# Projection's head: x turned, scaled and split tile by tile, beside the projection of its rows

## The chip, the cores and the metric

The kernel runs on one core of a Trainium2 chip. The metric is the device time of one execution in microseconds (us). The engines are TensorE (PE; its weight loads are shown as PEld), VectorE (DVE), ScalarE (ACT), GpSimd (POOL) and SyncE (SP), each with its own instruction stream; they wait for one another by semaphores. DMA queues move data between HBM and the on-chip memory (SBUF); matmul results lie in eight banks of PSUM.

## The reference

One inference step of one layer of a decoder: 512 prompt tokens and 8 x 8 sample tokens, 1024 channels.

```
h = rms_norm(x, g_attn) @ w_in        # 1024 -> 1816 columns
q, kv_c, kv_s, kv_w, gates, u = split(h)
# compressed, selected and window attention on q and kv (with paged caches),
# gated and added; trailing means of u through w_pool; joined
y = x + mix @ w_out
y = y + square(relu(rms_norm(y, g_mlp) @ w_up)) @ w_down
out = rms_norm(y, g_final)            # beside the new kv rows and states

def rms_norm(x, g):
    return x * rsqrt(mean(x * x) + eps) * g
```

Everything is 32-bit. The part that matters here is the first line: `rms_norm` and the columns kv_c, kv_s, kv_w and the gates of `w_in`.

## The kernel before

The work is staged: projection, compression of cached blocks, prompt attention, sample attention, MLP. The change lies in the head of the projection, the function `project`, and each engine's part of it is a nested function (`on_sync`, `on_scalar`, `on_vector`, `on_tensor`) whose order of writing is the order of execution on that engine.

The 576 tokens are five tiles: four of 128 prompt tokens and one of 64 sample tokens. x arrives with tokens on the partitions; matmuls need channels there. So PE turns each tile by 8 transposes of 128 channels each (L779), four into each of two banks of `pb[0]` to `pb[3]`. ACT keeps the first four channel groups in `hT` (L513) and DVE the other four (L643).

A product of 32-bit numbers is made of three matmuls in a shorter format (fp32r): each operand is split into a high half (a copy by ACT) and a low half (what is left, a subtraction by DVE), and high by high, high by low and low by high are added in one bank. Split are x times its gamma (`pxh` by L488, `pxl` by L571; one instruction each for a channel group k over all 576 tokens) and the weights of the row columns, which come in two groups: a (384 columns) and b (408). Group a comes as two loads of four channel groups, `rows_araw`; L484 makes `rows_ah`, L566 `rows_al`, one instruction for each half. The gammas come as rows (`colrows`), are turned by PE (L784) and kept by DVE (L647) as `cols`.

`project_rows(r)` (L753) projects one token tile on one column group: r = 0 to 4 are the five tiles on group a, r = 5 to 9 on group b. It is called pass r here; it has 8 channel groups of 3 matmuls and fills bank `pb[4 + r % 4]`. Pass 4 takes the bank of pass 0 and therefore waits for ra_kept, which says that ACT has kept the rows of tile 0:

```
if r - 4 < TILES:
    pe.wait_ge(ra_kept, r - 3)
```

The factor 1/sqrt(mean(x * x) + eps) (`rstd`) is applied when the rows are kept: `keep_rows` on ACT for group a (L505, L506), on DVE for group b (L585 to L588). It comes from five squares with a sum on ACT, one for each tile (`square`, L479), a mean on DVE (L659), a square root on ACT (L535, with a table load ahead of it) and a reciprocal on DVE (L661). ACT does the squares of tiles 0 and 1 between the turned tiles, the other three behind the last split of x, and then the split of group b's first half ahead of keep_rows(0).

After group a PE sums a diagonal of rstd into all partitions (L793), projects group b, and then eight units of 128 columns (u and q) for all tokens at once (L766). SP issues the loads in the order written; the load of u's columns (`u_raw`, L425) takes x's place and waits for all five squares and all turned tiles.

Of the kernel before, what the change touches and what calls it, by code (L numbers as in the profile page):

```python
# [217 lines left out]
def place_project(nc, m):  # L218

    sb, a = placer(nc), addresses()  # L220
    low, zone = a["low"], a["zone"]
    m.x = sb("px", zone, [P, TILES, D])
    m.xh = sb("pxh", zone + 5120, [P, KT_D, TOK], F32R)
    m.xl = sb("pxl", a["mixT"], [P, KT_D, TOK], F32R)
    m.rows_h = [sb("rows_ah", low, [P, KT_D, RA], F32R), sb("rows_bh", low + 6144, [P, KT_D, RB], F32R)]
    m.rows_l = [sb("rows_al", low + 3072, [P, KT_D, RA], F32R), sb("rows_bl", zone + 9728, [P, KT_D, RB], F32R)]
    m.rows_raw = [sb("rows_araw", zone + 12992, [P, KT_D, RA]), sb("rows_braw", zone + 16064, [P, KT_D, RB])]
    m.junk = sb("pjunk", zone + 19328, [P, D])
    slots = [zone + 19328] + [low + 2048 * s for s in range(3)]
# [130 lines left out]
def project(nc, m, sems, sem):  # L360
# [12 lines left out]
    raw_turned, xt_act, xt_dve = sem("raw_turned"), sem("xt_act"), sem("xt_dve")  # L373
    xh_ready, xl_ready, wh_ready, wl_ready = sem("pxh_ready"), sem("pxl_ready"), sem("pwh_ready"), sem("pwl_ready")
    UNIT0 = 4
# [16 lines left out]
    NU = 8  # L392

# [11 lines left out]

    def on_sync(sp):
        sp.dma_start(m.consts[:, 0:P], m.c_small[:, 0:P]).then_inc(ident_in, 16)
        for i in range(PTILES):
            sp.dma_start(m.x[:, i, :], m.x_prompt[0, P * i:P * i + P, :]).then_inc(x_in[i], 16)
        sp.dma_start(m.x[NS:P, PTILES, :], m.x_sample.rearrange("b t d -> (b t) d")).then_inc(x_in[PTILES], 16)  # L410
# [3 lines left out]
        wv = m.w_in_d[0].rearrange("(k p) n -> p k n", p=P)  # L414
        for c, (a, b) in enumerate(((KV0, KV0 + RA), (KV0 + RA, U0))):
            for h in range(2):
                sp.dma_start(m.rows_raw[c][:, 4 * h:4 * h + 4, :], wv[:, 4 * h:4 * h + 4, a:b])\
                  .then_inc(rowsw_in[c][h], 16)
            if c == 0:
                sp.dma_start(m.consts[:, P:], m.c_small[:, P:]).then_inc(sems.const_in, 16)  # L420
# [9 lines left out]
        sp.wait_ge(wl_ready, 4)  # L430
# [46 lines left out]
    def on_scalar(act):  # L477
# [4 lines left out]
        def split_rows(c, h):  # L482
            act.wait_ge(rowsw_in[c][h], 16)
            act.activation(m.rows_h[c][:, 4 * h:4 * h + 4, :], m.rows_raw[c][:, 4 * h:4 * h + 4, :], ACT.Copy)\  # L484
               .then_inc(wh_ready, 1)

        def split_x(k):
            act.activation(m.xh[:, k, :], m.hT[:, k, :], ACT.Identity, scale=ga[:, k:k + 1]).then_inc(xh_ready, 1)  # L488
# [20 lines left out]

        act.wait_ge(norm_step, CLEAR)  # L510
        for i in range(TILES):
            act.wait_ge(raw_turned, 2 * i + 1)
            act.activation(m.hT[:, 0:4, P * i:P * i + rows(i)],  # L513
                           pb[(2 * i) % 4][:, :].rearrange("p (k t) -> p k t", k=4)[:, :, 0:rows(i)], ACT.Copy)\
               .then_inc(xt_act, 1)
            if i < 2:
                if i:
                    act.wait_ge(ss_ready, i)
                square(i)
        act.wait_ge(cols_step, COLS_KEPT)  # L520
        act.wait_ge(xt_act, TILES)
        split_x(0)
        split_rows(0, 0)
        for k in range(1, 4):
            split_x(k)
        act.wait_ge(xt_dve, TILES)
        split_x(4)
        split_rows(0, 1)
        for k in range(5, KT_D):
            split_x(k)  # L530
        for i in range(2, TILES):
            act.wait_ge(ss_ready, i)
            square(i)
        act.wait_ge(norm_step, VAR)
        act.activation(rstd, var, ACT.Sqrt).then_inc(norm_step, 1)  # L535
        split_rows(1, 0)
        act.wait_ge(norm_step, RSTD)
        keep_rows(0)
        split_rows(1, 1)
# [21 lines left out]
    def on_vector(dve):  # L561
        steps = 0

        def split_rows(c, h):
            dve.wait_ge(wh_ready, 2 * c + h + 1)
            dve.tensor_tensor(m.rows_l[c][:, 4 * h:4 * h + 4, :], m.rows_raw[c][:, 4 * h:4 * h + 4, :],  # L566
                              m.rows_h[c][:, 4 * h:4 * h + 4, :].bitcast(F32), ALU.subtract).then_inc(wl_ready, 1)

        def split_x(k):
            dve.wait_ge(xh_ready, k + 1)  # L570
            dve.scalar_tensor_tensor(out=m.xl[:, k, :], in0=m.hT[:, k, :], scalar=ga[:, k:k + 1],  # L571
                                     in1=m.xh[:, k, :].bitcast(F32), op0=ALU.mult, op1=ALU.subtract)\
               .then_inc(xl_ready, 1)
# [67 lines left out]
        for i in range(TILES):  # L641
            dve.wait_ge(raw_turned, 2 * i + 2)
            dve.tensor_copy(m.hT[:, 4:8, P * i:P * i + rows(i)],  # L643
                            pb[(2 * i + 1) % 4][:, :].rearrange("p (k t) -> p k t", k=4)[:, :, 0:rows(i)])\
               .then_inc(xt_dve, 1)
        dve.wait_ge(cols_step, COLS_TURNED)
        dve.tensor_copy(m.cols[:, :], pb[7][:, 0:20]).then_inc(cols_step, 1)  # L647
        dve.wait_ge(xt_act, TILES)
        dve.wait_ge(xt_dve, TILES)
        dve.wait_ge(cols_step, COLS_KEPT)  # L650
        split_x(0)
        split_rows(0, 0)
        for k in range(1, 5):
            split_x(k)
        split_rows(0, 1)
        for k in range(5, KT_D):
            split_x(k)
# [9 lines left out]
        split_rows(1, 0)  # L667
        split_rows(1, 1)
# [65 lines left out]
    def on_tensor(pe):  # L734
        def project_rows(r):

            c, i = r // TILES, r % TILES
            t0 = P * i if i < PTILES else TOK - P
            if r >= 4:
                if r - 4 < TILES:  # L740
                    pe.wait_ge(ra_kept, r - 3)
                else:
                    pe.wait_ge(rb_rows, r - 3 - TILES)
            n = (RA, RB)[c]
            for k in range(KT_D):
                if r == 0:
                    pe.wait_ge(xl_ready, k + 1)
                if i == 0 and k % 4 == 0:
                    pe.wait_ge(wl_ready, 2 * c + k // 4 + 1)
                xh, xl = m.xh[:, k, t0:t0 + P], m.xl[:, k, t0:t0 + P]  # L750
                wh, wl = m.rows_h[c][:, k, :], m.rows_l[c][:, k, :]
                for part, (x, w) in enumerate(((xh, wh), (xh, wl), (xl, wh))):
                    last = pe.matmul(pb[4 + r % 4][:, 0:n], x, w, start=(k == 0 and part == 0),  # L753
                                     stop=(k == KT_D - 1 and part == 2))
            last.then_inc(rows_mm, 1)
# [13 lines left out]

        pe.wait_ge(ident_in, 16)  # L770
        for u in range(2 * TILES):
            i, kk = u // 2, u % 2
            if kk == 0:
                pe.wait_ge(x_in[i], 16)
            if u >= 4:
                pe.wait_ge((xt_act, xt_dve)[kk], i - 1)
            lo = first(i)
            for k in range(4):
                last = pe.transpose(pb[u % 4][:, P * k:P * k + rows(i)],  # L779
                                    m.x[lo:P, i, P * (4 * kk + k):P * (4 * kk + k) + P], ident[lo:P, lo:P])  # L780
            last.then_inc(raw_turned, 1)

        pe.wait_ge(cols_step, COLS_IN)
        pe.transpose(pb[7][:, 0:20], m.colrows[:, :], ident[0:20, 0:20]).then_inc(cols_step, 1)  # L784
        for r in range(TILES):
            if r == 3:
                pe.wait_ge(cols_step, COLS_KEPT)
            project_rows(r)
        pe.wait_ge(sems.cleared, 2)
        pe.wait_ge(rb_step, DIAG)  # L790
        pe.wait_ge(xt_act, TILES)
# [59 lines left out]
def compress(nc, m, sems, sem):  # L851
# [1334 lines left out]
```

## Time and profile before

| | us |
|---|---|
| median of 3 runs | 901.14 |
| lowest and highest | 899.55, 901.77 |
| the profiled execution's own time | 906.76 |
| its span, first to last instruction | 904.9 |
| PE busy in the span | 827.1 |
| DVE busy | 418.0 |
| ACT busy | 335.5 |

The profile is of one execution. All times in it count from the start of the span, and its durations belong to the 906.76, not to the median. "PEclk" or the clock column is the clock granted to PE: 1.00 is 2.4 GHz, 0.50 is 1.2 GHz. A row of a timeline gives start, duration, engine, line, operation, what is written and read, the count, and in brackets how long the engine was idle before and what ended that.

### The profile page before, as it was taken

The page shows a single profiled execution, that of the slowest core. Times are in us where ns is not written, and L with a number is a line of the kernel's source. Part 1 is how long each engine was busy: PE and PEld are TensorE (multiplying, and loading weights), DVE is VectorE, ACT ScalarE, POOL GpSimd, SP SyncE. Part 2 cuts the span into 40 slices and gives each one's busy share as a digit, 9 for nine tenths or more (in the row PEclk, how much of TensorE's full clock was granted, in tenths as well). Part 3 has the DMA queues.
Part 4 walks back from the last instruction along what each step waited for, and adds up shares of the span by engine and source line. Part 5 has one row for each costly group of instructions (what it writes and reads, how often), then busy time and mean ns, then how long its engine had stood idle before and what let it go on. Part 6 is the DMA issues. An engine that isn't in the chain of part 4 may idle for free.

```text
span 904.9 us, 18147 instructions
## 1 busy us (share of the span) xinstructions
PE 827.1 (91%) x7775; PEld 755.0 (83%) x7775; DVE 418.0 (46%) x782; ACT 335.5 (37%) x626; POOL 135.2 (15%) x160
## 2 busy tenths in 40 slices
PE   5999998987888867786999999999999999999995
PEld 4999977775555645465999999999999999999995
DVE  5435646664555475565327433344333433243432
ACT  6511155552566565463225431133212331043311
POOL 0001101100785345520220000000000000000120
PEclk8999999998899889896999999999999999999998
DMA  8912638932461206526221122222221122222002
GB/s 299 323 72 95 192 78 243 302 120 93 140 204 32 83 1 234 208 62 176 94 93 47 50 90 93 93 93 93 93 84 38 63 93 93 93 94 93 1 1 105
DMA packets 48793, 103.03 MB, mean 114 GB/s; under 512 B 7498, under 2 KB 19166, under 8 KB 46429
## 3 DMA queue, kind: packets, MB, share of 16 engines
q1 hardware_dynamic: 41821, 68.61, 22.9%
q0 software_dynamic: 6912, 33.56, 10.9%
q8 instruction: 45, 0.74, 0.3%
q14 instruction: 15, 0.12, 0.0%
HBM read 97.75 MB, written 8.53 MB: 117 GB/s over the span
## 4 chain that ended last, share of the span: by engine, by line
PE 55%; DVE 3%; issue 2%; POOL 2%; DMA 1%; ACT 1%; another core or an unknown queue 1%; SPq 0%; DVEq 0%; ACTq 0%; POOLq 0%
PE banks L1846 51%; PE banks L1662 1%; DMA low<-in_w_out 1%; POOL rowsT L1437 1%; POOL zone L1437 1%; DVE qT L1560 0%; PE banks L2068 0%; PE banks L1730 0%; DVE qT L1561 0%; PE banks L1651 0%; DVE qT L1568 0%; DVE zone L1572 0%; DVE qT L1565 0%; PE banks L1632 0%
## 5 line engine op out<-in xcount | busy, mean ns | idle before, releaser
L1846 PE MATMUL banks<-xh,wh 128*128 128x288 f32 x640 | 139.0, 299 | 5.4 <-DVE xl L1838 5.0
L1846 PE MATMUL banks<-xl,wh 128*128 128x288 f32 x640 | 138.6, 299 | 0.0
L1846 PE MATMUL banks<-xh,wl 128*128 128x288 f32 x640 | 138.5, 298 | 0.0
L1826 ACT ACTIVATE wh<-low 128x1024 fp32r<-128x1024 f32 x72 | 75.0, 1049 | 109.8 <-PE banks L1846 102.8
L1846 PE MATMUL banks<-ah,wh 128*128 128x288 f32 x512 | 110.1, 297 | 0.0
L1846 PEld LDWEIGHTS banks<-xh,wh 128*128 128x128 f32 x640 | 104.6, 191 | 6.2 <-issue 3.2
L1846 PE MATMUL banks<-ah,wl 128*128 128x288 f32 x512 | 109.7, 296 | 0.0
L1846 PE MATMUL banks<-al,wh 128*128 128x288 f32 x512 | 109.6, 296 | 0.0
L1846 PEld LDWEIGHTS banks<-xl,wh 128*128 128x128 f32 x640 | 104.8, 192 | 0.0
L1846 PEld LDWEIGHTS banks<-xh,wl 128*128 128x128 f32 x640 | 104.6, 191 | 0.0
L1993 DVE TENSOR_TENSOR hT<-banks,hT 128x288 f32<-128x288 f32 x64 | 26.3, 453 | 138.8 <-PE banks L1846 138.8
L1831 DVE TENSOR_TENSOR wl<-low,wh 128x1024 fp32r<-128x1024 f32 x72 | 87.4, 1216 | 5.1 <-ACT wh L1826 5.1
L1846 PEld LDWEIGHTS banks<-ah,wl 128*128 128x128 f32 x512 | 82.5, 189 | 0.0
L1846 PEld LDWEIGHTS banks<-al,wh 128*128 128x128 f32 x512 | 82.4, 189 | 0.0
L1846 PEld LDWEIGHTS banks<-ah,wh 128*128 128x128 f32 x512 | 82.4, 189 | 0.0
L1933 ACT ACTIVATE mixT<-mixT 128x576 f32<-128x576 f32 x32 | 22.0, 687 | 152.1 <-DVE mixT L1989 152.1
L1989 DVE SCALAR_TENSOR_TENSOR mixT<-banks,mixT 128x288 f32<-128x288 f32 x64 | 26.3, 453 | 103.6 <-PE banks L1846 103.4
L1902 POOL TENSOR_TENSOR mixT<-mixT,low 128x576 f32<-128x576 f32 x6 | 9.6, 1592 | 406.0 <-ACT low L1944 406.0
L963 DVE TENSOR_TENSOR blkl<-banks,blkh 128x512 fp32r<-128x512 f32 x64 | 41.2, 685 | 18.9 <-ACT blkh L920 18.7
L1154 ACT ACTIVATE zone<-banks,small 128x512 f32<-128x512 f32 (+3 forms) x64 | 33.2, 523 | 31.3 <-DVE small L1190 31.0
L920 ACT ACTIVATE blkh<-banks 128x512 fp32r<-128x512 f32 x64 | 34.8, 598 | 25.2 <-PE banks L1029 25.2
L1140 POOL TENSOR_SCALAR zone<-zone,small,gates 128x512 f32<-128x512 f32 (+3 forms) x64 | 39.0, 618 | 32.7 <-DVE small L1196 32.3
(341 smaller groups left out, 1374.0 us busy)
## 6 DMA issues: line engine op xcount, KB each, us to landing
low<-in_w_up SPq DMA_DIRECT2D x8, 2048.0 KB, 8.2
low<-in_w_down SPq DMA_DIRECT2D x8, 2048.0 KB, 7.8
zone<-in_cmp_w SPq DMA_DIRECT2D x16, 256.0 KB
o_swin<-in_state_win SPq DMA_DIRECT2D x8, 504.0 KB
px<-in_x_prompt SPq DMA_DIRECT2D x4, 512.0 KB, 5.2
u_raw<-in_w_in SPq DMA_DIRECT2D x1, 2048.0 KB, 10.0
q_raw<-in_w_in SPq DMA_DIRECT2D x1, 2048.0 KB, 10.3
low<-in_state_win SPq DMA_DIRECT2D x4, 512.0 KB
```

Of the source, the lines that this page charges most:

```text
L920: act.activation(m.blkh[u % RING][:, r, :], pb[4 + 2 * (u % 2) + r][:, :], ACT.Copy).then_inc(blk_hi, 1)
L963: dve.tensor_tensor(m.blkl[u % RING][:, r, :], pb[4 + 2 * (u % 2) + r][:, :], m.blkh[u % RING][:, r, :].bitcast(F32), ALU.subtract).then_i ...
L1140: last = pool.tensor_scalar(m.cp[v % 4][:, g, 0:width(v)], m.cp[v % 4][:, g, 0:width(v)], su(v)[:, g:g + 1], m.gates[:, tile(v), a:a + 1], ...
L1154: last = act.activation(m.cp[v % 4][:, g, 0:width(v)], pb[2 * (v % 2) + g][:, 0:width(v)], ACT.Exp, bias=nm(v)[:, g:g + 1], scale=-1.0, ac ...
L1437: pool.tensor_tensor(m.sp[n % 2][:, 512 * x:512 * x + 512].rearrange("p (m b q) -> p m b q", m=4, b=8), bigconst(m, "s_slc")[:, 512 * x:51 ...
L1826: act.activation(wcols(m.wh, i), raw_cols(i), ACT.Copy).then_inc(wh_ready, 1)
L1831: dve.tensor_tensor(wcols(m.wl, i), raw_cols(i), wcols(m.wh, i).bitcast(F32), ALU.subtract)\
L1846: last = pe.matmul(out(i, hf), w[wi], half(x[:, k, :], hf), start=first and part == 0, stop=end and part == 2)
L1902: pool.tensor_tensor(sqsum, sqsum, m.sq[n % 2], ALU.add).then_inc(sq_added, 1)
L1933: act.activation(m.act[i % 2], m.relu[i % 2], ACT.Square).then_inc(a_ready, 1)
L1989: op = dve.scalar_tensor_tensor(out=half(m.relu[i % 2], hf), in0=out(i, hf), scalar=0.0, in1=half(m.rb, hf), op0=ALU.max, op1=ALU.mult)
L1993: op = dve.tensor_tensor(h, out(i, hf), h, ALU.add)
```

## The change

On PE, tile 0 is turned, then the gammas, then tile 1; after that each pass r of group a is followed by the turning of tile r + 2, up to tile 4. ACT keeps both banks of a turned tile (tile 0's second half is kept by DVE). DVE multiplies the whole tile by the gammas into `xg`, which takes the room of mixT; ACT copies it to `pxh`, DVE subtracts into `pxl`, for all 8 channel groups of one tile in one instruction. Group a's weights are split in four quarters of two channel groups, two quarters between the steps of tile 0 and of tile 1 each. The squares of tiles 0, 1 and 2 stand on ACT behind the splits of tiles 2, 3 and 4, those of tiles 3 and 4 behind these. SP issues tile 0, the gammas, the first half of the weights, tile 1, the second half, the other tiles, group b, and then the rest of the constants. UNIT0, the count of weight splits ahead of the units, goes from 4 to 6.

```
@@ on_sync @@
         sp.dma_start(m.consts[:, 0:P], m.c_small[:, 0:P]).then_inc(ident_in, 16)
-        for i in range(PTILES):
-            sp.dma_start(m.x[:, i, :], m.x_prompt[0, P * i:P * i + P, :]).then_inc(x_in[i], 16)
-        sp.dma_start(m.x[NS:P, PTILES, :], m.x_sample.rearrange("b t d -> (b t) d")).then_inc(x_in[PTILES], 16)
+        load_x(0)
         for a, src in ((0, m.g_attn), (8, m.g_mlp), (16, m.pool_scale)):
...
+        load_rows(0, 0)
+        load_x(1)
+        load_rows(0, 1)
+        for i in range(2, PTILES):
+            load_x(i)
+        sp.dma_start(m.x[NS:P, PTILES, :], m.x_sample.rearrange("b t d -> (b t) d")).then_inc(x_in[PTILES], 16)
+        for h in range(2):
+            load_rows(1, h)
+        sp.dma_start(m.consts[:, P:], m.c_small[:, P:]).then_inc(sems.const_in, 16)
@@ on_scalar @@
+        def keep_x(i):
+            for kk in range(2 if i else 1):
+                act.wait_ge(raw_turned, 2 * i + kk + 1)
+                act.activation(m.hT[:, 4 * kk:4 * kk + 4, tokens(i)], turned(i, kk), ACT.Copy).then_inc(xt_act, 1)
+
+        def split_x(i):
+            act.wait_ge(xg_ready, i + 1)
+            act.activation(m.xh[:, :, tokens(i)], m.xg[:, :, tokens(i)], ACT.Copy).then_inc(xh_ready, 1)
...
+        keep_x(0)
+        split_x(0)
+        for k in range(0, 4, 2):
+            split_rows(0, k, 2)
+        keep_x(1)
+        split_x(1)
+        for k in range(4, KT_D, 2):
+            split_rows(0, k, 2)
         act.wait_ge(norm_step, CLEAR)
...
         for i in range(2, TILES):
+            keep_x(i)
+            split_x(i)
+            if i > 2:
+                act.wait_ge(ss_ready, i - 2)
+            square(i - 2)
+        for i in range(TILES - 2, TILES):
             act.wait_ge(ss_ready, i)
             square(i)
         act.wait_ge(norm_step, VAR)
         act.activation(rstd, var, ACT.Sqrt).then_inc(norm_step, 1)
-        split_rows(1, 0)
+        split_rows(1, 0, 4)
         act.wait_ge(norm_step, RSTD)
         keep_rows(0)
@@ on_vector @@
+        def scale_x(i):
+            dve.wait_ge(xt_act, 2 * i + 1)
+            dve.tensor_tensor(m.xg[:, :, tokens(i)], m.hT[:, :, tokens(i)],
+                              ga.unsqueeze(2).broadcast_to([P, KT_D, rows(i)]), ALU.mult).then_inc(xg_ready, 1)
+
+        def split_x(i):
+            dve.wait_ge(xg_ready, i + 1)
+            dve.wait_ge(xh_ready, i + 1)
+            dve.tensor_tensor(m.xl[:, :, tokens(i)], m.xg[:, :, tokens(i)],
+                              m.xh[:, :, tokens(i)].bitcast(F32), ALU.subtract).then_inc(xl_ready, 1)
...
+        scale_x(0)
         split_x(0)
+        for k in range(0, 4, 2):
+            split_rows(0, k, 2)
+        scale_x(1)
+        for k in range(4, KT_D, 2):
+            split_rows(0, k, 2)
+        split_x(1)
+        for i in range(2, TILES):
+            scale_x(i)
+            split_x(i)
         dve.wait_ge(ss_ready, TILES)
@@ on_tensor @@
+        turn_x(0)
         pe.wait_ge(cols_step, COLS_IN)
         pe.transpose(pb[7][:, 0:20], m.colrows[:, :], ident[0:20, 0:20]).then_inc(cols_step, 1)
+        turn_x(1)
         for r in range(TILES):
             if r == 3:
                 pe.wait_ge(cols_step, COLS_KEPT)
             project_rows(r)
+            if r + 2 < TILES:
+                turn_x(r + 2)
```

ACT before, from the last split of x to the first rows kept (pjunk is the squares' output, pxh the high half of x, rowsT the kept rows; in brackets the semaphores waited for):

```order
L488 ACTIVATE pxh<-hT,cols 128x576 [waits xt_dve]
L484 ACTIVATE rows_ah<-rows_araw 128x1536 [waits rowsw_in01]
L488 ACTIVATE pxh<-hT,cols 128x576 x3
L479 ACTIVATE pjunk,small<-px 128x1024 [waits ss_ready] x2
L479 ACTIVATE pjunk,small<-px 64x1024 [waits ss_ready]
L535 ACT_TABLE_LOAD
L535 ACTIVATE small<-small 128x5 [waits norm_step]
L484 ACTIVATE rows_bh<-rows_braw 128x1632 [waits rowsw_in10]
L505 ACTIVATE rowsT<-banks,small 128x256 [waits rows_mm,norm_step]
```

ACT after the change, from tile 3's turned halves to the same point (hT is the turned x, mixT the scaled x):

```order
L507 ACTIVATE hT<-banks 128x4x128 [waits raw_turned] x2
L511 ACTIVATE pxh<-mixT 128x8x128 [waits xg_ready]
L497 ACTIVATE pjunk,small<-px 128x1024 [waits ss_ready]
L507 ACTIVATE hT<-banks 128x4x64 [waits raw_turned] x2
L511 ACTIVATE pxh<-mixT 128x8x64 [waits xg_ready]
L497 ACTIVATE pjunk,small<-px 128x1024 [waits ss_ready] x2
L497 ACTIVATE pjunk,small<-px 64x1024 [waits ss_ready]
L552 ACT_TABLE_LOAD
L552 ACTIVATE small<-small 128x5 [waits norm_step]
L502 ACTIVATE rows_bh<-rows_braw 128x1632 [waits rowsw_in10]
L528 ACTIVATE rowsT<-banks,small 128x256 [waits rows_mm,norm_step]
```

In both, three squares stand between the last split of x and the square root; after the change the split ahead of them is that of tile 4, which waits for a turning (raw_turned) that PE makes behind pass 2.

PE before, from the last turned tile to pass 0:

```order
L779 MATMUL banks<-consts,px 128x64 [waits xt_act,x_in4]
L779 MATMUL banks<-consts,px 128x64 x3
L779 MATMUL banks<-consts,px 128x64 [waits xt_dve]
L779 MATMUL banks<-consts,px 128x64 x3
L784 MATMUL banks<-consts,colrows 128x20 [waits cols_step]
L753 MATMUL banks<-rows_ah,pxh 128x384 [waits pwl_ready,pxl_ready]
```

PE after, from the end of pass 2 over the turning of tile 4 to the start of pass 3:

```order
L775 MATMUL banks<-rows_al,pxh 128x384
L775 MATMUL banks<-rows_ah,pxl 128x384
L801 MATMUL banks<-consts,px 128x64 [waits xt_act,x_in4]
L801 MATMUL banks<-consts,px 128x64 x7
L775 MATMUL banks<-rows_ah,pxh 128x384 [waits pxl_ready,cols_step]
```

Tile 4's turning stood ahead of all passes and now stands behind the third. Pass 4 waits for ra_kept in both.

## Rows read from the trace of the kernel before

**Rows 1.** The page's busy time, share of the span, instructions.

```profile
PE 827.1 (91%) x7775; PEld 755.0 (83%) x7775; DVE 418.0 (46%) x782; ACT 335.5 (37%) x626; POOL 135.2 (15%) x160
```

**Rows 2.** Table by stretch: length, busy (count) of each engine, granted clock, DMA.

```profile
12.40:16.90 4.50, 0.02 (x1) 0.01 (x1) 3.10 (x5) 4.09 (x7) 0.00 (x0) 0.93 1.04 403
16.90:23.20 6.30, 5.88 (x18) 5.42 (x19) 6.30 (x8) 6.27 (x10) 0.00 (x0) 0.51 0.62 221
23.20:41.00 17.80, 17.80 (x104) 17.80 (x103) 6.98 (x14) 8.30 (x15) 0.00 (x0) 1.00 0.94 323
```

**Rows 3.** Waits of PE up to 140 us: total, times, longest.

```profile
PE banks L753 <- DVE rows_al L566: 4.9, 2, 4.5
```

**Rows 4.** Timeline of PE.

```profile
12.18 0.23 PE L784 MATMUL banks<-consts,colrows 20*128 20x20 f32 x1
16.92 0.66 PE L753 MATMUL banks<-rows_ah,pxh 128*128 128x384 f32 x1 [4.50 <-DVE rows_al L566]
...
20.26 0.52 PE L753 MATMUL banks<-rows_al,pxh 128*128 128x384 f32 x1
20.58 0.52 PE L753 MATMUL banks<-rows_ah,pxl 128*128 128x384 f32 x1
...
41.10 1.05 PE L793 MATMUL banks<-diag,ones 128*128 128x128 f32 x8
```

**Rows 5.** Timeline of ACT.

```profile
6.49 1.28 ACT L513 ACT_TABLE_LOAD   x1 [6.49 <-PE banks L779]
...
20.93 1.04 ACT L479 ACTIVATE pjunk<-px 128x1024 f32<-128x1024 f32 x1
...
24.44 1.28 ACT L535 ACT_TABLE_LOAD   x1
25.73 0.21 ACT L535 ACTIVATE small<-small 128x5 f32<-128x5 f32 x1
25.84 1.56 ACT L484 ACTIVATE rows_bh<-rows_braw 128x1632 fp32r<-128x1632 f32 x1
27.31 0.45 ACT L505 ACTIVATE rowsT<-banks,small 128x256 f32<-128x256 f32 x1
27.66 0.35 ACT L506 ACTIVATE rowsT<-banks,small 128x128 f32<-128x128 f32 x1
...
32.95 0.47 ACT L505 ACTIVATE rowsT<-banks,small 128x256 f32<-128x256 f32 x1 [2.85 <-PE banks L753]
...
37.13 0.47 ACT L505 ACTIVATE rowsT<-banks,small 128x256 f32<-128x256 f32 x1 [3.45 <-PE banks L753]
```

**Rows 6.** Timeline of DVE.

```profile
7.29 0.69 DVE L643 COPY hT<-banks 128x512 f32<-128x512 f32 x1 [6.43 <-PE banks L779]
9.00 0.69 DVE L643 COPY hT<-banks 128x512 f32<-128x512 f32 x1 [1.01 <-PE banks L779]
10.16 0.69 DVE L643 COPY hT<-banks 128x512 f32<-128x512 f32 x1 [0.47 <-PE banks L779]
...
12.63 0.17 DVE L647 COPY cols<-banks 128x20 f32<-128x20 f32 x1
```

**Rows 7.** Single lines, ns: shortest, median, longest; first and last start.

```profile
L513 ACT ACTIVATE hT<-banks x5: 384/594/607, 7.8 to 12.0; 128x512 f32<-128x512 f32 x4, 128x256 f32<-128x256 f32 x1
...
L499 ACT ACTIVATE unit_h<-u_raw x4: 1044/1046/1061, 42.1 to 44.9; 128x1024 fp32r<-128x1024 f32 x4
...
L577 DVE TENSOR_TENSOR unit_l<-u_raw,unit_h x4: 1211/1214/1216, 43.3 to 57.0; 128x1024 fp32r<-128x1024 f32 x4
...
L484 ACT ACTIVATE rows_ah<-rows_araw x2: 1467/1467/1467, 13.5 to 17.6; 128x1536 fp32r<-128x1536 f32 x2
```

**Rows 8.** DMA issues: count, KB each, median us to landing; one SP row.

```profile
px<-in_x_prompt SPq DMA_DIRECT2D x4, 512.0 KB, 5.2
u_raw<-in_w_in SPq DMA_DIRECT2D x1, 2048.0 KB, 10.0
...
rows_araw<-in_w_in SPq DMA_DIRECT2D x2, 768.0 KB, 8.4
...
4.65 0.29 SPq L413 DMA_DIRECT2D colrows<-in_pool_scale  x1
```

**Rows 9.** Waits of PE from 100 to 300 us: total, times, longest.

```profile
PE banks L1029 <- DMA zone<-in_cache_cmp,idx_cmp: 3.9, 3, 2.3
```

More of the change, by code:

```diff
@@ L224, in place_project @@
     m.xl = sb("pxl", a["mixT"], [P, KT_D, TOK], F32R)
+    m.xg = m.mixT
     m.rows_h = [sb("rows_ah", low, [P, KT_D, RA], F32R), sb("rows_bh", low + 6144, [P, KT_D, RB], F32R)]
@@ L372, in project @@
     DIAG, RB_SUMMED, RB_KEPT = 1, 2, 3
-    raw_turned, xt_act, xt_dve = sem("raw_turned"), sem("xt_act"), sem("xt_dve")
+    raw_turned, xt_act, xt_dve, xg_ready = sem("raw_turned"), sem("xt_act"), sem("xt_dve"), sem("xg_ready")
     xh_ready, xl_ready, wh_ready, wl_ready = sem("pxh_ready"), sem("pxl_ready"), sem("pwh_ready"), sem("pwl_ready")
-    UNIT0 = 4
+    RA_STEPS, UNIT0 = 4, 6
     rows_mm, ra_kept, rb_rows, unit_mm, tile_kept = (
@@ L392, in project @@
     NU = 8
+    sems.all_split = UNIT0 + NU
     def raw_unit(u):
@@ L404, in half, with tokens, turned, load_x @@
         return v[:, HALF * hf:HALF * hf + HALF]
+    def tokens(i):
+        return slice(P * i, P * i + rows(i))
+    def turned(i, kk):
+        return pb[(2 * i + kk) % 4][:, :].rearrange("p (k t) -> p k t", k=4)[:, :, 0:rows(i)]
     def on_sync(sp):
+        wv = m.w_in_d[0].rearrange("(k p) n -> p k n", p=P)
+        def load_x(i):
+            sp.dma_start(m.x[:, i, :], m.x_prompt[0, P * i:P * i + P, :]).then_inc(x_in[i], 16)
+        def load_rows(c, h):
+            a, b = ((KV0, KV0 + RA), (KV0 + RA, U0))[c]
+            sp.dma_start(m.rows_raw[c][:, 4 * h:4 * h + 4, :], wv[:, 4 * h:4 * h + 4, a:b])\
+              .then_inc(rowsw_in[c][h], 16)
         sp.dma_start(m.consts[:, 0:P], m.c_small[:, 0:P]).then_inc(ident_in, 16)
-        for i in range(PTILES):
-            sp.dma_start(m.x[:, i, :], m.x_prompt[0, P * i:P * i + P, :]).then_inc(x_in[i], 16)
-        sp.dma_start(m.x[NS:P, PTILES, :], m.x_sample.rearrange("b t d -> (b t) d")).then_inc(x_in[PTILES], 16)
+        load_x(0)
         for a, src in ((0, m.g_attn), (8, m.g_mlp), (16, m.pool_scale)):
@@ L413, in on_sync @@
             sp.dma_start(m.colrows[a:a + n, :], src.rearrange("l (k p) -> (l k) p", p=P)).then_inc(cols_step, 16)
[L414 to L420, printed above, removed]
+        load_rows(0, 0)
[7 more added lines that the diff above has]
+        sp.dma_start(m.consts[:, P:], m.c_small[:, P:]).then_inc(sems.const_in, 16)
         sp.dma_start(m.tab[:, :], m.page_table.rearrange("(o b) n -> o (b n)", o=1).broadcast_to([P, P]))\
@@ L429, in on_sync @@
         sp.dma_start(m.w2[:, :, :], m.cmp_w2[0].rearrange("c h d -> h c d")).then_inc(sems.w2_in, 16)
-        sp.wait_ge(wl_ready, 4)
+        sp.wait_ge(wl_ready, UNIT0)
         sp.dma_start(m.q_raw[:, :, :], wv[:, :, Q0:Q0 + 512]).then_inc(qw_in, 16)
@@ L480, in square, with split_rows @@
                            accum_out=ss[first(i):P, i:i + 1]).then_inc(ss_ready, 1)
[L482 to L488, printed above, removed]
+        def split_rows(c, k, n):
+            act.wait_ge(rowsw_in[c][k // 4], 16)
+            act.activation(m.rows_h[c][:, k:k + n, :], m.rows_raw[c][:, k:k + n, :], ACT.Copy).then_inc(wh_ready, 1)
+        def keep_x(i):
[5 more added lines that the diff above has]
+            act.activation(m.xh[:, :, tokens(i)], m.xg[:, :, tokens(i)], ACT.Copy).then_inc(xh_ready, 1)
         def split_unit(u):
@@ L508, in keep_rows @@
                            scale=rstd[lo:P, i:i + 1]).then_inc(ra_kept, 1)
-        act.wait_ge(norm_step, CLEAR)
[L511 to L530, printed above, removed]
-        for i in range(2, TILES):
+        keep_x(0)
[6 more added lines that the diff above has]
+            split_rows(0, k, 2)
+        act.wait_ge(norm_step, CLEAR)
+        for i in range(2, TILES):
+            keep_x(i)
[4 more added lines that the diff above has]
+        for i in range(TILES - 2, TILES):
             act.wait_ge(ss_ready, i)
@@ L535, in on_scalar @@
         act.activation(rstd, var, ACT.Sqrt).then_inc(norm_step, 1)
-        split_rows(1, 0)
+        split_rows(1, 0, 4)
         act.wait_ge(norm_step, RSTD)
         keep_rows(0)
-        split_rows(1, 1)
+        split_rows(1, 4, 4)
         for i in range(1, TILES):
@@ L562, in on_vector, with split_rows @@
         steps = 0
[L564 to L573, printed above, removed]
+        def split_rows(c, k, n):
+            dve.wait_ge(wh_ready, RA_STEPS * c + k // n + 1)
+            dve.tensor_tensor(m.rows_l[c][:, k:k + n, :], m.rows_raw[c][:, k:k + n, :],
+                              m.rows_h[c][:, k:k + n, :].bitcast(F32), ALU.subtract).then_inc(wl_ready, 1)
+        def scale_x(i):
[7 more added lines that the diff above has]
+                              m.xh[:, :, tokens(i)].bitcast(F32), ALU.subtract).then_inc(xl_ready, 1)
         def split_unit(u):
@@ L640, in on_vector @@
         dve.memset(ss, 1.0).then_inc(norm_step, 1)
[L641 to L645, printed above, removed]
         dve.wait_ge(cols_step, COLS_TURNED)
         dve.tensor_copy(m.cols[:, :], pb[7][:, 0:20]).then_inc(cols_step, 1)
-        dve.wait_ge(xt_act, TILES)
-        dve.wait_ge(xt_dve, TILES)
+        dve.wait_ge(raw_turned, 2)
+        dve.tensor_copy(m.hT[:, 4:KT_D, tokens(0)], turned(0, 1)).then_inc(xt_dve, 1)
         dve.wait_ge(cols_step, COLS_KEPT)
+        dve.wait_ge(xt_dve, 1)
+        scale_x(0)
         split_x(0)
[L652 to L657, printed above, removed]
+        for k in range(0, 4, 2):
[7 more added lines that the diff above has]
+            split_x(i)
         dve.wait_ge(ss_ready, TILES)
@@ L666, in on_vector @@
            .then_inc(rb_step, 1)
-        split_rows(1, 0)
-        split_rows(1, 1)
+        split_rows(1, 0, 4)
+        split_rows(1, 4, 4)
         dve.wait_ge(table_in, 16)
@@ L745, in project_rows @@
             for k in range(KT_D):
[L746 to L749, printed above, removed]
+                if c == 0 and k == 0:
+                    pe.wait_ge(xl_ready, i + 1)
+                if i == 0 and k % (2, 4)[c] == 0:
+                    pe.wait_ge(wl_ready, RA_STEPS * c + k // (2, 4)[c] + 1)
                 xh, xl = m.xh[:, k, t0:t0 + P], m.xl[:, k, t0:t0 + P]
@@ L768, in project_unit, with turn_x @@
             last.then_inc(unit_mm, 1)
-        pe.wait_ge(ident_in, 16)
[L771 to L781, printed above, removed]
+        def turn_x(i):
+            pe.wait_ge(x_in[i], 16)
+            if i >= 2:
+                pe.wait_ge(xt_act, 2 * i - 3)
+                if i == 2:
+                    pe.wait_ge(xt_dve, 1)
+            lo = first(i)
+            for kk in range(2):
+                for k in range(4):
+                    last = pe.transpose(pb[(2 * i + kk) % 4][:, P * k:P * k + rows(i)],
+                                        m.x[lo:P, i, P * (4 * kk + k):P * (4 * kk + k) + P], ident[lo:P, lo:P])
+                last.then_inc(raw_turned, 1)
+        pe.wait_ge(ident_in, 16)
+        turn_x(0)
         pe.wait_ge(cols_step, COLS_IN)
         pe.transpose(pb[7][:, 0:20], m.colrows[:, :], ident[0:20, 0:20]).then_inc(cols_step, 1)
+        turn_x(1)
         for r in range(TILES):
@@ L788, in on_tensor @@
             project_rows(r)
+            if r + 2 < TILES:
+                turn_x(r + 2)
         pe.wait_ge(sems.cleared, 2)
         pe.wait_ge(rb_step, DIAG)
-        pe.wait_ge(xt_act, TILES)
+        pe.wait_ge(xt_act, 2 * TILES - 1)
         for i in range(PTILES):
@@ L885, in on_gpsimd @@
             if ck == 1:
-                pool.wait_ge(sems.wl_ready, 12)
+                pool.wait_ge(sems.wl_ready, sems.all_split)
                 pool.wait_ge(sems.unit_mm, 5)
```

## The prediction

> **What bounds the kernel now.** Read the page's busy shares first: TensorE (PE) is busy for 91% of the span, and no other engine for half of it [rows 1]. So time is to be had only where PE stands still or runs at half its clock. The table by stretch, read next, shows one such place in the head of the projection, the first 41 us: from 12.4 to 16.9 us PE does nothing, and from 16.9 to 23.2 us it works at a granted clock of 0.51 (the 1.2 GHz level), after which the clock is 1.00 [rows 2]. The list of waits says what ended the idle time: the low half of the first row weights, rows_al, from VectorE (DVE) [rows 3]. The timeline of PE gives the marks that the sum hangs on: the last turning at 12.18, the first projection matmul at 16.92, the end of the first row group (five tiles, 24 matmuls each) at 41.10 [rows 4]. From there the second row group follows without a gap, so whatever moves the mark at 41.10 moves what comes after it.
>
> The reader should also see what ScalarE (ACT) does while PE is in tiles 0 and 1: it squares x (three of the five squares lie from 20.93 to 24.4), loads the square-root table, and at 27.31 starts to keep tile 0's rows with the factor rstd. It then waits for PE at 32.95 and 37.13: PE never waits for it [rows 5]. One pass of PE over a tile is 37.13 less 32.95, 4.18 us, or 0.174 us a matmul. Pass 4 thus began at 41.10 less 4.18, 36.92.
>
> **The first tile (a gain on PE).** Tile 0 is turned as before: DVE sees both halves at 7.29 [rows 6]. ACT's first table load has no wait on the turning any more (it stood at 6.49 for 1.28 us [rows 5]); that ends nothing later than DVE's own copies do, so I give it no term. Now in series: the turned gammas copied (0.17), tile 0's second half copied (0.69) [rows 6], to about 8.4 with PE's column turning ahead of them; scaled over 1024 numbers a partition (1.21), copied high by ACT (1.05), subtracted by DVE (1.21) [rows 7], each with about 0.1 to hand over: 12.1. ACT makes the two weight quarters beside DVE's subtraction; of 768 numbers each, they are estimated between the rows of nearest size at 0.85 on ACT and 0.95 on DVE [rows 6, 7], so DVE has the first at 13.1 and the second at 14.0. PE's first matmul comes at 13.2 instead of 16.92.
>
> The other two quarters come late, since ACT serves tile 1 ahead of them: keep tile 1 (2 x 0.59 from 12.4) to 13.6, DVE scales to 15.3, ACT splits to 16.4, and then quarters three and four. DVE has them at 18.3 and 19.3. PE's last six matmuls of pass 0 end at 19.4 + 6 x 0.174 = 20.5 at full clock. PE has a gap of some 3 us in this pass; if its clock is at half there (0.32 a matmul, see below), pass 0 ends at 22.3, and with tile 2's turning slower too the delay is 2.5. I take the full clock, because the gap is shorter than the 4.5 us in which it fell before, and keep 0 to 2.5.
>
> **Passes and turnings between them (no wait).** A turning is 1.1 us, from 9.00 to 10.16 [rows 6]. While PE makes a pass and a turning, 5.3 us, the two engines finish the next tile: 0.6 + 1.2 + 1.05 + 1.2 and four hand-overs, 4.5 us. So pass 2 ends at 20.5 + 2 x (1.1 + 4.18) = 31.1. Their cover is 0.8 us a tile; if it were gone, each tile would cost what it lacks.
>
> **What is late next: rstd (a new wait of PE).** ACT's squares 2, 3 and 4 now stand behind tile 4's split, in ACT's own order. Tile 4 is turned only after pass 2. Pass 4 must wait until tile 0's rows have left its bank, and that keeping needs rstd, which needs all five squares. From the end of pass 2: turn tile 4 and hand it over 0.7; keep its second half 0.4 (the shortest of the copies [rows 7]); scale 512 numbers 0.7; split 0.6; with hand-overs 2.5. Three squares, 20.93 to 24.44: 3.5. Table load and square root, 24.44 to 25.84: 1.4. The high copy of the second row group's first half, 25.84 to 27.31: 1.5, since it stands ahead of the keeping on ACT. The keeping, 27.31 to 28.02: 0.7 [rows 5]. Together 9.6, with a last hand-over 9.7. In this time PE has tile 4's turning and pass 3, 0.7 + 4.18 = 4.9. PE waits 4.8 us, and pass 4 starts at 31.1 + 9.7 = 40.8 instead of 36.92: **+3.9 us**, with all that was gained at the first matmul already in it. Queued behind that wait on PE is everything else; nothing of it can pass.
>
> The table load in this chain was hidden before. Its row is 1.28 us and the square root follows at once [rows 5]. The Trainium skill, "ScalarE: Activation LUTs", section "What ACT_TABLE_LOAD costs", says that a switch of table sets takes a drain of 1.38 us more, 2.66 in all. By that page the wait would be 1.4 longer and the sum below 8.0, thus 909.1; the trace doesn't agree, and I go by the row.
>
> **The clock behind that wait.** Before, PE stood for 4.5 us and its clock was at half when it came back, for 18 matmuls [rows 2]. They start 0.32 apart there [rows 4] instead of 0.174: 18 x 0.146 = 2.6 us lost. A stand of 4.8 us is as long, so I charge the same again: **+2.6**. The ends are 0 (the clock stays) and 2.8 (half for the full 6.3 us of that stretch). The old loss at 16.9 is inside the old mark and needs no term.
>
> **What costs nothing.** The loads: tile 0 is still the first large one. The small gamma rows are issued ahead of the weights now; how long they take to land has no row, only that PE turned them at 12.18, 7.5 us after the last was issued, without waiting [rows 4, 8]. Issued at about 2.5, that bounds them at 10.0, 2.7 late for the copy of the gammas; by the median of x, 5.2 from issue [rows 8], they are there at 7.7, which is 0.3. I take 0 and keep 2.7. The first weight half is issued some 2 us earlier and behind one x tile in place of five; by its old 8.4 from issue it lands at 11.4 at the latest, needed at 10.8: 0 to 0.6, and by bytes ahead of it 0. The second group's weights are behind the x tiles as before and needed 10 us later than before. The load of u_raw waits for the last square, so it is issued at about 37 and not 24.5, and lands 10.0 later [rows 8], at 47; its split on DVE is only needed by the unit passes behind five passes of the second group (22 us). q_raw and the state copies move behind it, into a stretch where loads are few.
>
> **Sum.** 3.9 + 2.6 = +6.5 us. The profiled execution's span of 904.9 would become 911.4 and its own time, 906.76, 913.3; that execution is 5.6 above the median of the runs, 901.14 (899.55 to 901.77), so the forecast for the median is 907.6.
>
> **Rivals.**
> First, the wait without the clock: PE stands for 4.8 us but comes back at 2.4 GHz. For it: in the old stand the clock kept its full level for most of the 4.5 us (mean 0.93 [rows 2]) and fell only near its end, so that a stand of this length may also get by. Against it: that one did not. 901.1 + 3.9 = 905.0.
> Second, a worse head: late gammas or the half clock in pass 0, +2.5 on top: 910.1. For it: pass 0 has two gaps, and the second eight transposes went at 0.21 us each (7.29 to 9.00) and the third at 0.145 (9.00 to 10.16) [rows 6].
> Third, on the other side: rstd isn't late. If keeping tile 0 were done within the 4.9 us that PE has after pass 2, the mark would be 31.1 + 4.9 + 4.18 = 40.2 instead of 41.1, thus 900.2. It decides at 4.9 us against my 9.7; the squares alone would have to vanish and the table load as well. Little speaks for it, since every duration but the short split is a row.
> Fourth, the shift is taken up later: the compression stage waits for gathered pages, 3.9 us in all [rows 9]. If they were there in time whatever PE does, 6.5 would shrink to 2.6: 903.7. Against it: those gathers are themselves issued on PE's progress, so they shift too.
>
> **Chances.** The forecast 0.60, the wait without the clock 0.23, the worse head 0.10, no late rstd 0.03, taken up later 0.04. What a measurement of this kernel can tell from no change is about 0.3%, 2.7 us, thus 898.4 and 903.8. Slower: 0.60 + 0.10 + most of 0.23, 0.89. Same: the fourth, most of the third, and a small part of the first where the head comes earlier than worked out, 0.09. Faster: 0.02. The range, 903.6 to 910.6, holds the wait without the clock a microsecond early and the worse head, and leaves out the third case.
>
> **What would show it.** Right: PE's first projection matmul near 13; two gaps in pass 0, each ended by rows_al; a wait of about 5 us of PE on ACT's keeping of rows at the fifth pass, the largest of the head; the granted clock near 0.5 for some 6 us behind it; the last three squares between about 34 and 37 on ACT. Wrong: no wait at the fifth pass, or one ended by another writer; a tile of x late at passes 1 to 3; the second group starting before 45 us.

## The result, and the profile after

The changed kernel takes 907.99 us (median of 14 executions, 903.02 to 912.74) against 903.03 for the kernel before (14 executions, 899.55 to 906.48). The ratio on record is 1.0069, with a 95% interval of 1.0047 to 1.0090. By it the change costs 6.2 us, by the difference of the two medians 5.0; 6.5 were forecast. A second comparison gave 1.0070 (1.0037 to 1.0102). The ratios leave out executions that are over 1.5% above the fastest of their kernel; two of the runs below lose some by it.

From the list of PE's waits in the first 140 us of the changed kernel (total, times, longest); the second line was not there before:

```profile
PE banks L801 <- DMA px<-in_x_prompt: 7.4, 2, 4.7
PE banks L775 <- ACT rowsT L529: 4.5, 1, 4.5
PE banks L775 <- DVE rows_al L583: 1.5, 2, 1.0
```

The wait for rows_al, 4.9 before [rows 3], has shrunk to 1.5; a wait of 4.5 for ACT's kept rows has come. PE's timeline gives the place of each (these rows answer to [rows 4]):

```profile
4.73 1.94 PE L801 MATMUL banks<-consts,px 128*128 128x128 f32 x8 [4.73 <-DMA px<-in_x_prompt]
6.60 0.29 PE L808 MATMUL banks<-consts,colrows 20*128 20x20 f32 x1
9.52 1.97 PE L801 MATMUL banks<-consts,px 128*128 128x128 f32 x8 [2.62 <-DMA px<-in_x_prompt]
12.47 0.66 PE L775 MATMUL banks<-rows_ah,pxh 128*128 128x384 f32 x1 [0.98 <-DVE rows_al L583]
...
17.20 0.69 PE L775 MATMUL banks<-rows_ah,pxh 128*128 128x384 f32 x1 [0.55 <-DVE rows_al L583]
...
21.05 1.03 PE L801 MATMUL banks<-consts,px 128*128 128x128 f32 x8
...
31.26 0.71 PE L801 MATMUL banks<-consts,px 64*128 64x64 f32 x8
...
40.84 0.45 PE L775 MATMUL banks<-rows_ah,pxh 128*128 128x384 f32 x1 [4.50 <-ACT rowsT L529]
...
46.70 1.05 PE L820 MATMUL banks<-diag,ones 128*128 128x128 f32 x8
...
48.04 0.46 PE L775 MATMUL banks<-rows_bh,pxh 128*128 128x408 f32 x1
```

The first projection matmul comes 4.45 us earlier than before (12.47 for 16.92), pass 0 ends at 21.05, pass 2 at 31.26. Then pass 4 starts at 40.84 and group a ends at 46.70, 5.6 later than the 41.10 of before. ACT's timeline shows the chain that holds pass 4 (it answers to [rows 5]):

```profile
33.17 0.63 ACT L511 ACTIVATE pxh<-mixT 128x512 fp32r<-128x512 f32 x1 [0.76 <-DVE mixT L588]
33.71 1.05 ACT L497 ACTIVATE pjunk<-px 128x1024 f32<-128x1024 f32 x1
...
36.05 1.05 ACT L497 ACTIVATE pjunk<-px 64x1024 f32<-64x1024 f32 x1
...
37.22 1.28 ACT L552 ACT_TABLE_LOAD   x1
38.51 0.21 ACT L552 ACTIVATE small<-small 128x5 f32<-128x5 f32 x1
38.63 1.55 ACT L502 ACTIVATE rows_bh<-rows_braw 128x1632 fp32r<-128x1632 f32 x1
40.08 0.45 ACT L528 ACTIVATE rowsT<-banks,small 128x256 f32<-128x256 f32 x1
40.44 0.35 ACT L529 ACTIVATE rowsT<-banks,small 128x128 f32<-128x128 f32 x1
```

From tile 4's split to the kept rows ACT is without a gap: split, three squares, table load, root, weight split, keeping. The table by stretch (columns as in [rows 2]) shows PE's stand, the time in which it does nothing, and the clock behind it:

```profile
36.50:40.50 4.00, 0.00 (x0) 0.00 (x0) 1.60 (x5) 3.97 (x7) 0.00 (x0) 1.00 0.53 140
41.20:44.70 3.50, 3.50 (x13) 3.50 (x12) 3.21 (x5) 2.92 (x7) 0.00 (x0) 0.52 1.06 401
44.70:48.00 3.30, 3.30 (x22) 3.15 (x21) 1.13 (x5) 1.08 (x3) 0.00 (x0) 0.99 1.13 290
```

The granted clock is at half from about 41.2 to 44.7 us; it fell just after PE had gone on at 40.84. Pass 4 takes 46.70 less 40.84, 5.86 us, where 4.18 is its time at full clock: 1.7 us.

### The profile page after: what moved, and what is told of

It is laid out like the page before. It is cut to its first block, busy times and chain, and to the rows that moved or that the text cites. A ratio compares the mean times of both kernels' runs of the same rounds, so it can differ in the third digit from the quotient of the medians.

```text
span 909.6 us, 18154 instructions
## 1 busy us (share of the span) xinstructions
PE 826.9 (91%) x7775; PEld 755.2 (83%) x7775; DVE 421.0 (46%) x782; ACT 337.0 (37%) x629; POOL 134.0 (15%) x160
## 4 chain that ended last, share of the span: by engine, by line
PE 54%; DMA 3%; POOL 2%; DVE 2%; issue 2%; ACT 1%; SPq 0%; DVEq 0%; ACTq 0%; POOLq 0%
PE banks L1873 51%; DMA low<-in_w_out 1%; DMA low<-in_cache_slc,idx_slc 1%; PE banks L1689 1%; POOL zone L1464 1%; DMA zone<-in_cache_slc,idx_slc 1%; POOL low L350 1%; POOL zone L350 1%; PE banks L1757 0%; POOL rowsT L1464 0%; PE banks L2095 0%; PE banks L1708 0%; PE banks L1730 0%; PE banks L1659 0%; DVE y L2052 0%
## 5 line engine op out<-in xcount | busy, mean ns | idle before, releaser
L990 DVE TENSOR_TENSOR blkl<-banks,blkh 128x512 fp32r<-128x512 f32 x64 | 41.2, 686 | 11.2 <-ACT blkh L947 10.9
L1689 PE MATMUL banks<-consts,zone 128*128 128x128 f32 x160 | 29.1, 334 | 16.1 <-ACT zone L1433 7.9
```

The source lines that it names most:

```text
L990: dve.tensor_tensor(m.blkl[u % RING][:, r, :], pb[4 + 2 * (u % 2) + r][:, :], m.blkh[u % RING][:, r, :].bitcast(F32), ALU.subtract).then_i ...
L1689: last = pe.transpose(pb[6 + u % 2][:, P * mm:P * mm + P], m.kst[(UN * n + u) % 3][:, P * mm:P * mm + P], ident)
```

## The experiments

My theory was that the whole loss is the late rstd, with the clock behind its wait. The rivals were that the turnings between the passes or the half clock of pass 0 cost the time, or that the wait doesn't matter in the end. The mark used below is the start of group b on PE: 42.45 before, 48.04 after. Ratios are to the kernel before, run beside each; the executions of one kernel spread over 7 to 12 us. A mark is from the one profiled execution of a run, a time is the median of some twelve.

**The squares moved.** On ACT of the changed kernel:

```
-            if i > 2: act.wait_ge(ss_ready, i - 2)
-            square(i - 2)              # behind split_x(i), i = 2, 3, 4; then 3 and 4; then the root
+        squares of tiles 0 to 3        # ahead of keep_x(2), each waiting for its x
+        square of tile 4               # behind split_x(2)
+        square root                    # behind split_x(3); DVE's mean and reciprocal to match
```

> The changed kernel with ScalarE's order altered: the squares of tiles 0 to 3 stand ahead of tile 2's turned halves, the square of tile 4 behind tile 2's split, the square root behind tile 3's split (VectorE's mean and reciprocal moved to match). Theory 1 (the loss is the late rstd alone, with the clock behind it): TensorE does not wait at the fifth pass, or under 0.5 us; the second column group starts near 42.0 us instead of 48.0; the time is 0.5 to 1 us under the kernel before, ratio about 0.999. Rival (the loss comes from the turnings between the passes or from the half clock in the first pass, and the wait only shows it): the second group still starts 3 us or more later than in the kernel before, ratio 1.004 or more.

Measured: 903.09, ratio 0.9994 (0.9971 to 1.0017). PE's waits up to 70 us and the mark:

```profile
PE banks L808 <- DMA px<-in_x_prompt: 7.5, 2, 4.9
PE banks L782 <- DVE rows_al L588: 2.0, 2, 1.0
PE banks L782 <- DVE pxl L599: 0.9, 1, 0.9
```

```profile
41.33 0.45 PE L782 MATMUL banks<-rows_bh,pxh 128*128 128x408 f32 x1
```

The wait at pass 4 is gone, and with it the whole loss, while all turnings still stand between the passes. The rival of the turnings falls. The squares now hold up tile 2 a little (0.9, for its low half, at pass 2). The mark is 1.1 earlier than before, but the time is not lower. In this execution only the first nine matmuls of pass 0 start 0.32 apart, so this run alone doesn't rule out the half clock there; the changed kernel run again, below, does. Run once more:

> The run with the squares moved once more, on the same chip as the other three: 0.998 to 1.000, by a second group that starts 1 us earlier than in the kernel before.

Measured: 903.13, ratio 1.0010 (0.9984 to 1.0035), mark 41.29.

**The squares late in the kernel before.** One line:

```
+        act.wait_ge(rows_mm, 3)
         for i in range(2, TILES):
             act.wait_ge(ss_ready, i)
             square(i)
```

> The kernel before with one wait added: ScalarE does the squares of tiles 2, 3 and 4 only once TensorE has ended its third pass. Nothing else of the change is in it. Theory 1: this alone makes the kernel slower; TensorE waits about 3.3 us at the fifth pass (third pass ends near 32.9; squares 3.5, root 1.4, copy 1.5, keeping 0.7), and loses 0 to 2.6 us by the clock behind it: +3.3 to +5.9 us, ratio 1.0035 to 1.0065. Rival: the wait is made up for later (by pages that are then there in time), ratio under 1.002.

Measured: 908.02, ratio 1.0050 (1.0020 to 1.0080), mark 47.66. From the list of waits and, below, the table by stretch:

```profile
PE banks L754 <- ACT rowsT L506: 3.0, 1, 3.0
```

```profile
41.50:44.50 3.00, 3.00 (x11) 3.00 (x11) 2.72 (x5) 2.23 (x7) 0.00 (x0) 0.50 1.08 387
```

Late squares alone make the old kernel as slow as the changed one, within the intervals: 3.0 us of stand, then the clock at half, 40.46 to 46.32 for pass 4, 5.86 us again. (0.5 of the 5.2 by which the mark is later is x, which landed at 5.79 and not 5.32.)

**The stand filled.** Between pass 3 and pass 4 of the changed kernel:

```
+            if r == 4:
+                for n in range(26):
+                    pe.matmul(pb[3][:, 0:RA], m.xh[:, n % 8, 0:P], m.rows_h[0][:, n % 8, :], start=True, stop=True)
             project_rows(r)
```

> The changed kernel with 26 matmuls of no use (384 columns, into a bank that is free) on TensorE between the fourth and the fifth pass: they take 26 x 0.172 = 4.5 us, as long as the wait, so that TensorE does not stand still there. If the clock falls because of the stand (my term of 2.6 us): the granted clock stays at 1.00 after 36 us, the fifth pass takes 4.2 us instead of 5.9, and the second group starts near 46.4 instead of 48.0; the time is 1.5 to 2.6 us under the changed kernel, about 1.004 times the kernel before. Rival (the clock falls here whatever TensorE does, or its fall costs nothing): same as the changed kernel, 1.007.

Measured: 905.65, ratio 1.0030 (1.0004 to 1.0056), mark 46.66. The clock stays whole over the place of the stand and behind it:

```profile
36.50:40.50 4.00, 4.00 (x25) 4.00 (x24) 1.41 (x5) 3.97 (x6) 0.00 (x0) 1.00 0.48 117
40.50:45.00 4.50, 4.50 (x27) 4.18 (x26) 4.22 (x5) 3.81 (x9) 0.00 (x0) 1.00 1.06 398
```

```profile
41.03 0.44 PE L775 MATMUL banks<-rows_ah,pxh 128*128 128x384 f32 x1
...
45.32 1.05 PE L823 MATMUL banks<-diag,ones 128*128 128x128 f32 x8
```

Pass 4 takes 4.29 us, against 5.86. The clock's part is so 1.6 us by that pass, 1.4 by the mark, and 2.3 by the medians (907.99 less 905.65, of two separate comparisons whose intervals overlap). What is left is the wait without the clock: 4.2 by the mark, 2.6 by the medians.

**The keeping ahead of the split.** On ACT `keep_rows(0)` moved ahead of `split_rows(1, 0, 4)`.

> The changed kernel with the keeping of tile 0's rows ahead of the split of the second group's first half on ScalarE. The chain behind the last squares loses that split (1.5 us) but must then wait for VectorE's reciprocal (0.4): theory 1 gives a wait of 3.4 us instead of 4.5 at the fifth pass, and the clock may or may not fall: -1.1 us to -3 against the changed kernel, 1.004 to 1.006 times the kernel before. If the wait does not shrink, the chain I name is not what ends it.

Measured: 907.33, ratio 1.0049 (1.0028 to 1.0071); the wait and the clock behind it:

```profile
PE banks L775 <- ACT rowsT L529: 3.4, 1, 3.4
```

```profile
38.20:42.50 4.30, 4.25 (x24) 4.26 (x25) 3.04 (x3) 4.30 (x7) 0.00 (x0) 1.00 1.05 402
```

The wait shrank as worked out, so the chain is the one I named. In this one execution the clock didn't fall and pass 0 was faster too (mark 43.88). It is the fastest of the twelve, 903.45, so it doesn't show what the clock did in the others; the median, 0.7 less than the changed kernel's, can't be told from it.

**The weights first.** The squares early as above, and on ACT and DVE all four quarters ahead of tile 1:

```
-        for k in range(0, 4, 2): split_rows(0, k, 2)
+        for k in range(0, KT_D, 2): split_rows(0, k, 2)
         keep_x(1); split_x(1)          # on DVE: scale_x(1); split_x(1)
-        for k in range(4, KT_D, 2): split_rows(0, k, 2)
```

> The changed kernel with the squares early (as in the run with the squares moved) and, besides, all four weight quarters ahead of tile 1's scaling and split on ScalarE and VectorE. Theory: the gap in the first pass (1 us, ended by rows_al) goes, VectorE has the last quarter near 15.0 instead of 18.0 us; the first pass is then bound by its own half clock (24 x 0.32 = 7.7 us from 12.5 to 20.2, or less where the clock rises in it); the second group starts at 40 to 41 us against 42.5 in the kernel before; 1.5 to 2.5 us under the kernel before, ratio 0.997 to 0.998. Rival: tile 1 is then late for the second pass and takes the place of the gap: no better than with the squares moved alone, ratio 0.999.

Measured: 900.07, ratio 0.9952 (0.9926 to 0.9977), mark 39.92. The gap in the middle of pass 0 is gone, and tile 1 is in time; the only wait for a tile is 0.4, at pass 3.

**The head filled.** As that, and on PE 12 transposes of no use ahead of `turn_x(1)` and 5 behind it.

> As the run with the weights first, and TensorE is kept at work in the head: 12 transposes of no use between the turning of the gammas and that of tile 1, and 5 between tile 1 and the first pass, into a bank that is free. If the half rate of the first pass is the clock answering to TensorE's standing still, the matmuls of the first pass start 0.172 us apart instead of 0.32, the pass is bound by the weight quarters and ends near 16.5, and the second group starts near 39 us: 3 to 4 us under the kernel before, ratio 0.996. Rival: the rate of the first pass does not depend on what TensorE did before it; then this is the same as the run without the transposes.

Measured: 898.73 over six executions, mark 39.57. The ratio, 0.9876 (0.9808 to 0.9944), counts only three of them, since one was very short (885.47); so it was run again:

> The run with the weights first and the head filled once more, since few of its executions were counted: second group at 39.6, that is 2.9 us under the kernel before by the marks, ratio 0.997; if its first result (0.988) is to be repeated, something behind the head gains 8 us more, which no mark of the head shows.

Measured: 898.55, ratio 0.9949 (0.9922 to 0.9976), mark 39.12. Pass 0 in it:

```profile
12.68 0.41 PE L780 MATMUL banks<-rows_ah,pxh 128*128 128x384 f32 x1 [0.72 <-DVE rows_al L588]
12.93 0.34 PE L780 MATMUL banks<-rows_al,pxh 128*128 128x384 f32 x1
13.11 0.34 PE L780 MATMUL banks<-rows_ah,pxl 128*128 128x384 f32 x1
...
19.15 0.45 PE L780 MATMUL banks<-rows_ah,pxh 128*128 128x384 f32 x1 [1.18 <-DVE pxl L599]
```

The matmuls start 0.175 apart from the first on: the rate of pass 0 does hang on what PE did before. But pass 0, now over at 16.94, then waits for tile 1, and the mark is only 0.4 to 0.8 earlier than without the transposes. This version beats both kernels, with or without the filling.

**The head filled, weights as the change has them.** The squares moved and the same 17 transposes.

> The run with the squares moved, with the same 17 transposes of no use in the head, and the weight quarters where the change put them. It tells the clock from the weights: the first half of the first pass at 0.172 a matmul, but its second half still waits for rows_al until 17.2 and 18.1 us, so that the pass ends near 19.2 in every execution; the second group starts near 40.5 to 41.3; ratio to the kernel before 0.998 to 0.999.

Measured: 899.33, ratio 0.9941 (0.9913 to 0.9970), mark 42.30. Again:

> The run with the squares moved and the head filled once more. Its first result (0.994) is more than its mark allows (the second group started at 42.3, as in the kernel before). By the marks it should be 0.998 to 1.000; if 0.994 comes again, the gain lies behind the head.

Measured: 899.41, ratio 0.9954 (0.9927 to 0.9982), mark 41.49. The first mark was a miss: behind a wait of 2.40 for rows_al the second half of pass 0 ran at 0.32 a matmul, which I had not expected with the head filled; the second mark was as expected. The times are lower than the marks allow by some 3 us, both times. Where that comes from I could not settle: from the mark to the end single profiles differ by more than that, most of all in the compression stage (75 us from its first to its last turning in both profiles with the squares moved, 73 and 75 in these two, 78 in that of the kernel before), so single traces don't tell it. The record has the mean granted clock of each execution, and it goes with the time (correlation -0.9 over the 12 executions of either repeat). These had 0.964 on average, the repeat with the squares moved 0.9615; at the 0.6 to 0.8 us for each 0.001 that these executions show I estimate that about half of the difference of 3.7 us goes with the clock. In which stage is not shown.

**The changed kernel again**, unaltered:

> The changed kernel once more, unaltered, beside these on the same chip: the second pair of halves of the first pass at either rate (0.32 or 0.172 a matmul, up to 1.5 us), the wait of 4.5 us at the fifth pass in either case, the clock at half behind it for 0 to 6 us; ratio to the kernel before 1.005 to 1.009.

Measured: 908.42, ratio 1.0070 (1.0037 to 1.0102), wait 4.5, pass 4 from 39.73 to 45.58, 5.85 us, mark 46.93. In this execution the second half of pass 0 ran at full clock and the pass ended at 19.95, about as with the squares moved (19.52); the wait at pass 4 and the clock behind it were the same. So the half clock of pass 0 is not what makes the kernel slower.

**The head of the kernel before filled.** 30 transposes of the identity ahead of pass 0.

> The kernel before with 30 transposes of no use (the identity by itself, into a free bank) on TensorE between the turning of the gammas and the first pass, where it stood for 4.5 us. Nothing of the change is in it. It measures my clock term by itself. If the clock falls because of the stand: no matmul of the first pass at 0.32 us, the second group starts near 39.8 instead of 42.5, and the time is 2.6 us lower, ratio 0.997. Rival: the clock of the first pass does not hang on the stand: ratio 1.000, or above it if the transposes themselves are late.

Measured: 901.61, ratio 0.9980 (0.9956 to 1.0005), mark 41.93: 0.5 earlier, not 2.6, and 0.4 of that is x, which landed at 4.94 and not 5.32. By the mark a miss; the ratio can't tell 0.997 from 1.000. PE's timeline and, behind it, that of its weight loads show why:

```profile
16.98 0.34 PE L753 MATMUL banks<-rows_ah,pxl 128*128 128x384 f32 x1
17.18 0.45 PE L753 MATMUL banks<-rows_ah,pxh 128*128 128x384 f32 x1
...
17.64 0.34 PE L753 MATMUL banks<-rows_ah,pxl 128*128 128x384 f32 x1
17.91 0.45 PE L753 MATMUL banks<-rows_ah,pxh 128*128 128x384 f32 x1
...
21.13 0.41 PE L753 MATMUL banks<-rows_ah,pxh 128*128 128x384 f32 x1 [1.70 <-DVE rows_al L566]
```

```profile
17.18 0.19 PEld L753 LDWEIGHTS banks<-rows_ah,pxh 128*128 128x128 f32 x1 [0.19 <-DVE pxl L571]
17.91 0.19 PEld L753 LDWEIGHTS banks<-rows_ah,pxh 128*128 128x128 f32 x1 [0.25 <-DVE pxl L571]
```

At full clock PE waits for DVE at the channel groups (0.73 apart) and then for the second weights. The half clock of the old first pass stood mostly beside DVE's work and cost little.

## Why the prediction was right, point by point

- The time came closer than the sum: 907.6 forecast, 907.99 measured, but that is in part luck. The sum was put on the median of three executions of the kernel before, 901.14, where fourteen have 903.03, so the base was 1.9 too low. The loss, forecast at 6.5, is 5.0 by the medians, 5.6 by the mark and 6.2 by the ratio.
- The wait, the base of the forecast: worked out at 4.8, measured 4.5, ended by ACT's keeping of rows; pass 4 at 40.84 where 40.8 was worked out, +3.9. Shown necessary (squares moved) and enough (squares late in the kernel before).
- The clock behind it is the term that was mis-sized: 2.6 worked out, 1.7 measured in three executions (5.86, 5.86 and 5.85 for pass 4; 1.6 against the 4.29 of the filled run), none in a fourth (the keeping ahead of the split). I had carried over the 18 matmuls at half clock of [rows 2]; here some 12 were, from 41.2 to 44.7, 3.5 us and not some 6. The mark moved by 5.6, not 6.5; the interval of the time, 4.2 to 8.1 us, holds both.
- I said that the old loss at 16.9 was inside the old mark; the last run shows that it was hardly a loss, so that stretch was a poor measure of what the clock costs at pass 4, where nothing else holds PE.
- Pass 0: I took the full clock and 20.5. It ran at half from its start, and ended at 21.05 with x landing 0.6 earlier (4.73, not 5.32). My reason, that the gap is too short for the clock to fall, missed the point: tile 1's eight transposes took 1.97, where tile 2's took 1.03, so PE was at half already ahead of the pass. That pass 2 still ended near the 31.1 worked out is luck: a turning between passes took 0.8, not 1.1, which made up for it. The spacing in pass 0:

```profile
13.24 0.52 PE L775 MATMUL banks<-rows_ah,pxl 128*128 128x384 f32 x1
13.56 0.52 PE L775 MATMUL banks<-rows_ah,pxh 128*128 128x384 f32 x1
```

- The second half of that pass went at 0.32 or 0.174, by the execution (17.20 to 21.05 here, 17.73 to 19.95 in the changed kernel run again); that was the "worse head" rival, worth 1.6 us, in part.
- Passes 1 to 3 waited for no tile, as said. The turned gammas were not late (6.60). Tile 1 of x was: PE stood 2.62 us for it, which I had not worked out. It held nothing up, since ACT came to it only at 11.5.
- The rivals "rstd isn't late" and "the shift is taken up later": neither happened, as PE waited for rstd and the time rose about as much as the mark.
- The drain behind the table load that the Trainium skill, "ScalarE: Activation LUTs", "What ACT_TABLE_LOAD costs", names did not show here either: load at 37.22 for 1.28, root at 38.51. (1.4 on the sum of 6.5 would have been 7.9, not 8.0.)

## What to carry to other kernels

When work is moved to start a pipeline earlier, list what else the old order hid: here ACT did the last squares beside PE's pass 0 (20.93 to 24.4 [rows 5]), long before pass 4 needed them. In the new order they come late, and the gain of 4.45 us at the first matmul was paid back, and more, at the first place that needs their result. A short chain on an idle engine belongs where that engine waits, not behind the last step of the loop it shares. Charge a clock loss only where no other wait of the same stretch would have covered it.

## What the runs showed of the hardware

- The clock column reads 1.00 from the start of the span of the changed kernel, up to 41 us, although the matmuls of the first pass start 0.32 us apart, as they do where the column is at 0.50 (41.6 to 44.5; 0.174 at 1.00 behind that). Ahead of its first change that column did not show the half rate; read the spacing.
- The length of a stand does not by itself decide: after 3.0 us (squares late) the clock went to half, after 3.4 us (keeping first) it stayed at 1.00, and the matmuls 0.174 apart.
